# Delta rule: levels of one pair of chains among the last value projections, and decays from fetched rows of gate sums in place of decay products

## What is computed

```
gc = cumsum(g);  decay = exp(where(incl, gc_i - gc_j, -inf))
a = eye + where(strict, (k @ k.T) * decay * beta_i, 0)
u, w = solve(a, [v * beta, k * beta * exp(gc)])        # unit lower triangular
v_new = u - w @ S
o = (q * exp(gc)) @ S + where(incl, (q @ k.T) * decay, 0) @ v_new
S = S * exp(g_last) + (k * exp(g_last - gc)).T @ v_new
```

## Time and profile before

| | us |
|---|---|
| median of 3 runs (lowest to highest) | 4155.15 (4152.97 to 4157.54) |
| the profiled execution's own time | 4154.04 |
| its span | 4152.2 |
| its TensorE busy, share of the span | 3614.7 (87%) |
| DVE, ACT, POOL busy | 2494.0, 1018.3, 1231.7 |
| first half: end of job 12's products | 181.6 |
| first half: end of job 15's products | 205.0 |
| first half: last product of the chains | 470.6 |

### The profile page before, as it was taken

How to read it: one execution, slowest core, us unless ns; L and a number is a source line. 1 busy time by engine, 2 the same in 40 slices (tenths; PEclk the granted TensorE clock), 3 DMA queues, 4 the chain that set the end, 5 groups by cost and what they waited for, 6 DMA issues and landing times.

```text
span 4152.2 us, 58681 instructions
## 1 busy us (share of the span) xinstructions
PE 3614.7 (87%) x22496; PEld 1980.6 (48%) x22496; DVE 2494.0 (60%) x5805; ACT 1018.3 (25%) x2685; POOL 1231.7 (30%) x1262
## 2 busy tenths in 40 slices
PE   7978999789899977777888888887777889999999
PEld 3467544675544433233333445443222368655774
DVE  3457534564566677777688755667776348545341
ACT  2333213331222222223223542222222121010100
POOL 1054100540134444444444421444444010025000
PEclk9989999899999999999999999999999999999999
DMA  8200244001599999999999976999999334420443
GB/s 284 94 11 4 92 163 163 4 3 52 215 389 408 418 419 419 410 413 414 407 400 412 419 285 230 410 417 419 414 416 417 109 95 140 150 86 31 145 152 122
DMA packets 270111, 1043.61 MB, mean 251 GB/s; under 512 B 19931, under 2 KB 104166, under 8 KB 171530
## 3 DMA queue, kind: packets, MB, share of 16 engines
q0 software_dynamic: 115184, 815.62, 48.2%
q1 hardware_dynamic: 154650, 224.23, 16.0%
HBM read 1038.64 MB, written 1.13 MB: 250 GB/s over the span
## 4 chain that ended last, share of the span: by engine, by line
PE 55%; DMA 25%; DVE 10%; issue 3%; ACT 3%; POOL 2%; DVEq 0%; POOLq 0%; ACTq 0%
DMA arena<-in_peer_uv,arena 25%; PE psum L1912 12%; PE psum L267 11%; PE psum L305 7%; PE psum L780 5%; PE psum L1870 4%; DVE arena L2061 3%; PE psum L829 3%; PE psum L218 2%; PE psum L1149 1%; PE psum L1198 1%; PE psum L1209 1%; PE psum L515 1%; POOL arena L3534 1%; ACT arena L1950 1%
## 5 line engine op out<-in xcount | busy, mean ns | idle before, releaser
L1912 PE MATMUL psum<-arena 128*128 128x512 f32 x3072 | 1466.3, 620 | 331.1 <-ACT arena L1950 328.6
L2061 DVE SCALAR_TENSOR_TENSOR arena<-arena 128x1024 bf16<-128x1024 f32 x768 | 940.5, 1225 | 495.6 <-DMA arena<-in_peer_uv,arena 471.1
L2011 POOL DMA_INDIRECT arena<-in_peer_uv,arena x768 | 863.7, 1125 | 1180.3 <-PE psum L1912 1050.9
L1912 PEld LDWEIGHTS psum<-arena 128*128 128x128 f32 x3072 | 573.7, 195 | 1135.1 <-issue 566.6
L267 PE MATMUL psum<-ring,arena 128*128 128x512 f32 (+1 forms) x1088 | 461.2, 585 | 14.4 <-DVE arena L3347 4.4
L1943 ACT ACTIVATE arena<-arena 128x2 f32<-128x2 f32 x384 | 78.3, 204 | 1183.7 <-DVE arena L2061 1183.2
L267 PEld LDWEIGHTS psum<-ring,arena 128*128 128x128 f32 x1088 | 204.2, 191 | 266.5 <-issue 248.8
L1950 ACT ACTIVATE arena<-consts,arena 128x128 f32<-128x128 f32 x768 | 270.7, 394 | 223.9 <-DVE arena L2073 221.8
L305 PE MATMUL psum<-arena,ring 128*128 128x256 f32 x1408 | 305.3, 379 | 1.5 <-ACT arena L353 1.1
L305 PEld LDWEIGHTS psum<-arena,ring 128*128 128x128 f32 x1408 | 267.1, 190 | 37.6 <-ACT arena L353 1.7
L780 PE MATMUL psum<-arena,ring 128*128 128x512 f32 x512 | 229.0, 600 | 1.6 <-issue 1.6
(11 more groups left out here) (498 smaller groups left out, 4035.6 us busy)
## 6 DMA issues: line engine op xcount, KB each, us to landing
arena<-in_ada_w SPq DMA_DIRECT2D x48, 1024.0 KB, 7.0
ring<-in_ffn_w_up SPq DMA_DIRECT2D x44, 1024.0 KB, 5.0
ring<-in_dn_w_in SPq DMA_DIRECT2D x24, 1024.0 KB, 5.5
ring<-in_peer_w_query SPq DMA_DIRECT2D x22, 1024.0 KB, 9.3
ring<-in_ffn_w_down SPq DMA_DIRECT2D x20, 1024.0 KB, 4.9
arena<-in_peer_uv,arena POOLq DMA_INDIRECT x768, 12.7
ring<-in_ev_w_in SPq DMA_DIRECT2D x10, 1024.0 KB, 5.1
ring<-in_dn_w_out SPq DMA_DIRECT2D x8, 1024.0 KB, 4.7
```

Of the source, the lines that this page charges most:

```text
L1912: m = e.matmul(k.banks[4 + t % 2 * 2 + nh], self.diag[g % self.ND], self.vsl[g % self.NS][:, nh * 512:(nh + 1) * 512], start=u % 8 == 0 an ...
L2011: e.indirect_dma_start(self.uv[g % self.NS], None, self.table(), bass.IndirectOffsetOnAxis(ap=self.eid[u % 6][:, s:s + 1], axis=0)).then_i ...
L2061: e.scalar_tensor_tensor(self.junk[g % 2], self.us[g % self.NS], 1.0, self.h[:, u // 8, :], MUL, MUL, accum_out=self.a[u % 2][:, s:s + 1]) ...
```

## The change

- **Decays.** The decay products, DVE's mask multiplications and their waits go. `pe_sums` forms a fourth sum per tile and direction (32 small products in place of 24), the gates' sum measured from the middle of the tile; ACT copies it with either sign (`gcs`, `ngc`), TensorE turns it, DVE copies it, and SP stores it to DRAM in two arrangements (`sp_sums`, 13 transfers). For each chain and step SP fetches rows of it, broadcast over the partitions (`sp_rows`, five transfers). ACT makes the differences with eight Relus of 128x128 (`act_near`), each with a column of the sums as its bias, and takes Exp of minus the result, now from SBUF (`act_decay`). The Relus of the next step stand in phases 20 and 21. The fetched rows of a direction share one buffer (`rb`) between the two pairs.
- **Phases.** A step has 24 phases in place of 28, and the second pair runs 12 behind in place of 14.
- **The early levels.** The chains' order is turned, so that the first pair holds banks 4 to 7. Value columns are projected in the order 4 to 7, 0 to 3. Phases 0 to 11 of the first pair stand among the products of jobs 13, 14 and 15, one after every second product; on DVE they stand among the steps of convolutions 12 to 15, on ACT around evac and Silu. ACT makes the first pair's Relus and Exps of step 0 in one bundle after Silu 11, the second pair's after Silu 14 (`act_first`). Three more phases come before row 15. Keys are turned in jobs 11 and 12.
- **Moved.** POOL's multiplication of values by beta goes from the head of a step to the end of the one before. The z products use banks 4 to 7 first. Of the z weights three blocks are loaded before the later rows, one after them.

```diff
-            self.z[half].sp(e)
+            if half == 0:
+                self.sp_sums(e)
+            e.wait_ge(*self.P.at(("arow", half, len(self.LATE[half]) - 1)))
+            for ch in self.chains[0:2]:
+                self.sp_rows(e, half, 0, ch)
+            e.wait_ge(*self.V.at("cols1" if half else ("fin", 0, 1)))
+            for ch in self.chains[2:4]:
+                self.sp_rows(e, half, 0, ch)
+            self.z[half].sp(e, 0, 3)
+            e.wait_ge(*self.P.at(("rw", half, 15)))
+            for i in range(1, 4):
+                for ch in self.chains:
+                    hg, d = ch
+                    if not hg or i > 1:
+                        e.wait_ge(*self.S.at((half, i - hg, (1 - hg, d), "DT")))
+                        e.wait_ge(*self.S.at((half, i - hg, (1 - hg, d), "D")))
+                    self.sp_rows(e, half, i, ch)
+            self.z[half].sp(e, 3)
...
+    def sp_rows(self, e, half, i, ch):
...
+        if i:
+            e.wait_ge(*self.S.at((half, i - 1, ch, "x")))
+        e.dma_start(flat(plain), self.gc_d[n, ch[1], h0:h0 + 4].rearrange("h t -> (h t)").partition_broadcast(128)).then_inc(*lane.up())
+        for b, r in enumerate(self.quarters()):
+            e.dma_start(flat(near)[r], self.gn_d[n, ch[1], b, h0:h0 + 4].rearrange("h t -> (h t)").partition_broadcast(32),
+                        ).then_inc(*lane.up((half, i)))
...
     def pe(self, e):
...
                 for q in range(8):
                     m = e.matmul(self.job_bank(j), w[:, q, j % 2 * 128:(j % 2 + 1) * 128], self.hT[:, q, :], start=q == 0, stop=q == 7)
...
+                    if j >= self.EARLY and q % 2:
+                        next(turns)
...
+            for _ in range(3):
+                next(turns)
             self.pe_rows(e, half, 15)
...
     def act(self, e):
...
+                early = j - self.EARLY + 1
+                if early in (0, 1, 2):
+                    next(turns)
+                    next(turns)
+                elif early == 3:
+                    next(turns)
                 e.wait_ge(*self.V.at(("conv", half, j)))
                 dst = self.qT[:, n, :] if kind == "q" else self.cvs[j % 2]
                 e.activation(dst, self.cvs[j % 2], ACT.Silu, bias=0.0, scale=1.0).then_inc(*S.up(("silu", half, j)))
-            self.act_decay(e, half, 0, self.chains[0])
+                if early == -1:
+                    self.act_first(e, half, self.chains[0:2])
+                elif early == 2:
+                    e.wait_ge(*k.gates[half].at("all"))
+                    self.act_first(e, half, self.chains[2:4])
+                if early in (0, 1, 2):
+                    next(turns)
+                    next(turns)
+            for _ in range(3):
+                next(turns)
             self.act_rows(e, half, 15)
...
-    PHASES, LAG = 28, 14
+    PHASES, LAG = 24, 12
...
+    def act_near(self, e, half, i, ch):
...
+        e.wait_ge(*self.l_rb[ch].at((half, i)))
+        for h in range(4):
+            a, c = h0 + h, ch[1]
+            e.activation(near[:, h, :], near[:, h, :], ACT.Relu, bias=self.ngc[:, n, c, a:a + 1], scale=1.0).then_inc(*self.S.up())
+            e.activation(plain[:, h, :], plain[:, h, :], ACT.Relu, bias=self.gcs[:, n, c, a:a + 1], scale=-1.0,
+                         ).then_inc(*self.S.up((half, i, ch, "x")))
+
+    def act_decay(self, e, half, i, ch, name):
+        n = 1 if name == "DT" else 0
+        if i:
+            e.wait_ge(*self.P.at((half, i - 1, ch, "o" if n else "S")))
+        e.wait_ge(*self.S.at((half, i, ch, "x")))
+        e.activation(self.bufs[ch][1 + n], self.decay_in(i, ch)[n], ACT.Exp, bias=0.0, scale=-1.0).then_inc(*self.S.up((half, i, ch, name)))
```

More of the change, by code:

```diff
@@ L873, in pe_rows @@
         e.wait_ge(*self.S.at(("silu", half, j)))
-        if j >= 12:
-            e.wait_ge(*(self.S if j % 2 else self.V).at(("kTe", half, j - 12)))
+        if half == 0 and j == 10:
+            e.wait_ge(*self.V.at("gcr"))
+        if j == 15:
+            e.wait_ge(*self.V.at((half, 0, self.chains[1], "DTq")))
+        elif j >= 12:
+            e.wait_ge(*self.S.at(("rows", half, j - 1)))
+        elif j == 11:
+            e.wait_ge(*self.S.at(("evac", half, 11)))
         elif j >= 4:
-            e.wait_ge(*self.S.at(("rows", half, j - 4)))
+            e.wait_ge(*self.S.at(("rows", half, j - 2 if j == 10 else j - 4)))
         kind, c, n = self.jobs(half)[j]
@@ L1159, in pe_chain @@
         wide = lambda a: a.rearrange("p (h n) -> p h n", h=4)
+        late = pair[0] != self.chains[0]
         for i in range(4):
@@ L1162, in pe_chain @@
             key = lambda name, ch: (half, i, ch, name)
-            for name in ("DT", "D"):
-                for ch in pair:
-                    if not first:
-                        self.pe_decay(e, half, i, ch, (name,))
-                    yield
             for ch in pair:
@@ L1170, in pe_chain @@
                 bv = self.two(ch)[0][:, 0:256].rearrange("p (q n) -> p q n", q=2)
+                if not first:
+                    e.wait_ge(*V.at((half, i - 1, ch, "S")))
+                elif late:
+                    e.wait_ge(*S.at(("rows", half, 14) if ch[1] else ("evac", half, 14)))
+                else:
+                    e.wait_ge(*S.at(("kTe", half, 1)))
+                    e.wait_ge(*V.at(("kTe", half, 0)))
                 if i % 2 == 0:
-                    e.wait_ge(*S.at(key("D", ch)))
-                    if first:
-                        e.wait_ge(*S.at(("kTe", half, 3)))
-                        e.wait_ge(*V.at(("kTe", half, 2)))
                     for rows, cols, at in self.near():
@@ L1183, in pe_chain @@
                 b1, tok = self.two(ch)[1], self.place(half, ch, i)[1]
-                e.wait_ge(*S.at(key("DT", ch)))
+                if not first:
+                    e.wait_ge(*V.at((half, i - 1, ch, "O")))
+                elif late:
+                    e.wait_ge(*S.at(("evac", half, 15)))
+                    e.wait_ge(*V.at("cols1" if half else ("fin", 0, 1)))
                 for q in range(2):
@@ L1284, in pe_chain @@
                     e.wait_ge(*V.at(key("DTq", ch)))
+                    e.wait_ge(*S.at(("rows", half, 15)))
                 else:
@@ L1325, in turned, with act_first @@
                 for n, a in ((3, 0), (5, 128))]
-    def act_decay(self, e, half, i, ch, names=("DT", "D")):
-        for name in names:
-            n = 1 if name == "DT" else 0
-            e.wait_ge(*self.P.at((half, i, ch, name)))
-            e.activation(self.bufs[ch][1 + n], self.two(ch)[n].rearrange("p (h n) -> p h n", h=4), ACT.Exp, bias=0.0,
-                         scale=1.0).then_inc(*self.S.up((half, i, ch, name)))
+    def act_first(self, e, half, pair):
+        for ch in pair:
+            self.act_near(e, half, 0, ch)
+            for name in ("D", "DT"):
+                self.act_decay(e, half, 0, ch, name)
+    def act_near(self, e, half, i, ch):
+        n, tok, h0 = self.place(half, ch, i)
+        near, plain = self.decay_in(i, ch)
+        e.wait_ge(*self.l_rb[ch].at((half, i)))
[10 more added lines that the diff above has]
+        e.activation(self.bufs[ch][1 + n], self.decay_in(i, ch)[n], ACT.Exp, bias=0.0, scale=-1.0).then_inc(*self.S.up((half, i, ch, name)))
     def act_chain(self, e, half, pair):
@@ L1350, in act_chain @@
                 yield
+            for ch in pair if not first else ():
+                self.act_decay(e, half, i, ch, "DT")
             yield
@@ L1390, in act_chain @@
             yield
-            yield
-            yield
+            for ch in pair:
+                if i < 3:
+                    self.act_near(e, half, i + 1, ch)
+                yield
             yield
@@ L1438, in pool_chain @@
             yield
+            for ch in pair if first else ():
+                e.wait_ge(*S.at(("rows", half, 15 if late else 11)))
+                self.pool_values(e, half, 0, ch)
             yield
@@ L1468, in pool_chain, with pool_values @@
             yield
+            for ch in pair:
+                if i < 3:
+                    e.wait_ge(*(V.at(key("vb", ch)) if i else P.at(key("vn", ch))))
+                    self.pool_values(e, half, i + 1, ch)
+                yield
             yield
             yield
-            yield
-            yield
+    def pool_values(self, e, half, i, ch):
+        n, tok, h0 = self.place(half, ch, i)
+        e.tensor_tensor(self.bv[ch], self.vt[:, n, ch[0] * 4:ch[0] * 4 + 4, :],
+                        self.be[:, n, ch[1], h0:h0 + 4].unsqueeze(2).to_broadcast([128, 4, 128]), MUL).then_inc(*self.G.up((half, i, ch, "bv")))
     def dve_mod(self, e, half, j):
```

196 lines of the change are left out of this document (97 added, 99 removed).

## The result

The kernel after takes 4133.06 us (median of four runs, 4130.44 to 4138.19) beside 4156.34 for the kernel before on the same chip: a ratio of 0.9942, interval 0.9929 to 0.9955. Run again, unchanged, beside the last batch of experiments it took 4135.12 us against 4161.05 (0.9933, 0.9916 to 0.995). By the medians the change gives 23 to 26 us of the 48 forecast. The profiled execution is the slowest of the first four (4138.19 us, span 4136.4), and the profiled one of before was quick for its kernel (4154.04). So the two profiles differ by only 15.8 us: what follows shows 7 to 10 us less gain than the medians.

The account below looks back on a forecast made before the run. TensorE was taken to bound the touched Delta rule, with idle gaps and a lower clock in the seam. The sum -40 - 10.6 + 2.6 = -48 us took 4154.04 to 4106 us, range 4078 to 4140.

Parts of the forecast that it names:

- (b): Rival for the whole kernel: removed products leave open gaps, only 1 us gained a half-step; 4138 us, chance 0.25.
- Part 2: Steady stretch of seven half-steps: with 24 phases and lag 12, 2.85 us saved a half-step, 40 us in all.
- Part 3: Relus (2.3 us a chain-step) and row fetches (8.6 us a pair) in the steady stretch: both hide, fetches with 4 us to spare.
- Part 1: Decay products removed from TensorE: 27.4 us a half in the steady stretch, 9.1 us in the seam.
- gaps open: Low end for the steady stretch: gaps the products covered open wholly, leaving 1 us a half-step, 7 a half.
- The late X1: Every second half-step, X1 of the pair ahead waits for DVE: ready at 7.4 us where TensorE wants it at 6.
- second steady stretch: Seven half-steps of the second half, taken as 207.3 us beside 206.9 in the first, halves agreeing to 0.4 us.
- Part 4: Seam, from job 12's end to the first pair's X6: X6 at +54.5 for +59.8, 5.3 us a half, 10.6 in all.
- second bundle: ACT's bundle in the seam, forecast from +36.8 to +43.3 after job 12, with TensorE stalling 6 us.
- Part 5: One-time costs: added sums products +2.3 us on TensorE, +2.6 in the sum; first rows ready just in time.
- The table load: ACT's switch from Silu to Exp: 1.28 us by the row, against 2.66 with the skill's added drain.
- (a): Rival: TensorE's work is the whole limit of the steady stretch; gain 27 a half there, 10 a seam; 4083 us, chance 0.15.

Follow-up runs that it names:

- e8: Changed kernel without the row fetches of steps 1 to 3 (save one pair of chains at first), computing from stale rows: 4112.85 us, ratio to before 0.9887.
- e9: Changed kernel with all fetches on the bus, nearly all of steps 1 to 3 landing unread, computing from stale rows: 4129.76 us, ratio to before 0.9921.
- e7_cut: Kernel before, most decay products of steps 1 to 3 cut, phases and lag unchanged, Exp giving ones: 4168.04 us, ratio to before 1.0011.
- e5_swap: Changed kernel with TensorE and ScalarE taking the second pair's X6 and Y6 ahead of the first pair's X1 and Y1: 4140.04 us, ratio to before 0.9947.

## Why the prediction had the sign and half the gain

It forecast a gain, and there is one; the time lies inside the range (4133 in 4078 to 4140); the gain forecast is twice the measured one. The range held the time because it took in rival (b), not because the sum was right.

**The step that failed is Part 2, 20 us a half, 40 of the 48.** It added up the new half-step from durations of the old rows, taken at a clock of 0.98 and 0.96, and had no term for TensorE losing pace; Part 3 priced the new transfers at nothing for TensorE. Measured were 9.7 and 7.0 us, of which 3.4 each was only moved. The idle time came as forecast (36.2 and 39.7 us for 37), the busy time did not: 161 and 163 us for 150, at 0.87 and 0.85. With the transfers left out (e8) the stretches took 190.2 and 187.8 us, near the 187 forecast, and the transfers put back (e9) cost 17 us again.

By its own steps:

- **Part 1, the products go: right as a count, wrong as time.** 27 us of decay products left a half, TensorE's busy time fell by 17 and 18. The end of the range, "gaps open", had this possibility; the value taken did not. e7_cut shows it bare.
- **Part 2, in detail.** I never asked what else was spread over the 14 turns of the old lag: 3.4 us a half of z products left the stretch and came back behind the chains. They flatter the measured 9.7 and 7.0; in the whole they are no loss that a run shows. The late X1, for which I took off 2.3 us every second time, was no term of its own (e5_swap). My second steady stretch ended at 960.00; the X6 that ends it starts at 962.52, so the halves of before differed by 2.9 us and not by 0.4.
- **Part 3, Relus and fetches: the latency was right, the price was wrong.** Relus 2.4 us a chain-step; rows land 3.1 us after the issue; ACT waits for none. I priced the transfers by whether ACT gets them in time, and named SP's queue behind them, but not who else uses the DMA engines. They cost about 17 us, a third of the forecast gain, mostly in pauses in which TensorE had no instructions.
- **Part 4, the seam: waits right, sum 3 to 4 us off.** 1.2 and 2.5 us gained in place of 5.3 each. Key product a started at +8.1 (forecast +7.5), X1 at +18.7 (+15.4), Y4 at +37.7 (+35.5), X6 at +58.6 (+54.5). Most of the slip is there by X1: behind the first stall of 4.9 us four of job 13's instructions take 3.78 us where 1.98 is usual, at a granted clock of 0.50 (191 to 196). The second bundle came to 8.3 us (220.80 to 229.1), not 6.5: I had left its own table load out.
- **Part 5: 1.3 us for 2.6**, small (and its text works out 2.3, where the sum has 2.6). The first rows were in time: ACT's first Relu follows Silu 11 at once (181.62).
- **The table load**: 1.28 us, and the next activation 0.02 us after its end here (184.06 and 1.28, then 185.36). The Trainium skill ("ScalarE: Activation LUTs", What ACT_TABLE_LOAD costs) adds 1.38 us of drain; this trace does not show it.
- **The rivals**: (a) never came near. (b), gaps open and the clock falls, is what the trace shows beside my forecast, at 4138: the measured time is nearer to it than to 4106, and it deserved more than 0.25. Its gaps were partly others than I named: behind instructions, not only behind X5 and Y5.

By the medians 22 to 25 us are missing. The fetches (17) and the seams (6.9) come to 24. The first figure comes from medians whose intervals are 6 us to either side, the second from single profiles that differ by 2 to 3 us a stretch, so the fit is partly luck and the parts are known only to some 5 us.

## What to carry to other kernels

When work is taken off an engine, ask at which clock the rest will run: here cutting it in the old order gave nothing, and only an order that filled the waits gave time. Transfers into idle DMA time are not free when an engine runs hundreds of small instructions in microseconds; look for pauses without a semaphore, count the instructions up to them, and see whether they stand at one place of every 256. When a lag or phase count changes, list everything that is spread over its turns.

## What the runs showed of the hardware

- TensorE's instructions come in packets of 16 KB, one for 256 of them (175 for 44,800), every 4 to 5 us in the steady stretches. All 22 pauses without a semaphore there stood at one place of these blocks. The one followed lasted 0.55 us without fetches and 2.52 us behind a burst of them, and the products behind the long one took up to 1.8 times as long (2.08 us for 1.16).
- Removing TensorE work without closing its waits went with a lower granted clock (0.98 to 0.88) and a stretch longer than before (206.9 to 216.0 us); that run also worked on other numbers, which was not kept apart.
- 128x128 f32 activations from SBUF to SBUF: 0.39 us each in the trace, one every 0.29 us.
